# One kernel, one change: the second matrix of each expert as a single 4 MB load

## The chip, the cores and the metric

The kernel runs on one core of a Trainium2 chip. The metric is the time of one execution on the device in microseconds (us). Times of engines and transfers come from a hardware profile of one execution.

## What is computed

One decoder layer for 16 + 256 tokens of width 1024: attention and a state-space mixer side by side, gates, an output projection, and then the part that matters here, a layer of 32 experts of which every token takes 4. Cut to it:

```python
def moe_ffn(u, w_router, b_router, w1, b1, w2, b2):
    ...
    def body(acc, inp):
        tok, wt, e = inp
        hb = swiglu_clamped(u[tok] @ w1[e] + b1[e])     # w1[e]: 1024 x 2048
        yb = (hb @ w2[e] + b2[e]) * wt[:, None]         # w2[e]: 1024 x 1024
        return acc.at[tok].add(yb), None
```

`swiglu_clamped` takes the even columns of its input as one operand and the odd ones as the other, so 2048 columns give 1024 hidden units. All weights are float32: 8 MB for the first matrix of an expert, 4 MB for the second.

## The kernel before

Everything is held in SBUF: `ring`, 12 slots of 8 KB per partition, and `arena`, some 100 KB per partition. Each engine runs its own program; semaphores join them. All loads of weights are issued by SP, in one order written out by hand.

Up to about 480 us the kernel computes the projections, both mixers, the branch projections (`branch`, 12 groups counted by `branch_used`), the merged gates (`m_done`), the output projection (`wo_half` when its first half is through, `h_ready`) and the router. The weights of that part pass through slots 0 to 6 of the ring; slots 7 to 9 are scratch of the mixers and slots 10 and 11 hold the gates (`gsig`) until `m_done` is 8.

Then come the 32 experts in order, for up to 64 tokens each (`expert` of TensorE). An expert has six parts (`PARTS = 6`), each a load of 2 MB, that is 16 KB per partition (`BUF`): four parts of the first matrix (`w1_v`: part `s` has rows 256 s to 256 s + 255, two rows to a partition) and two halves of the second (`w2_v`: four rows to a partition). The first matrix has two sets of buffers: `even_bufs[0:4]` for even experts and `odd_bufs` for odd ones. The two halves of the second matrix have one buffer each, `even_bufs[4]` and `even_bufs[5]`, for all experts. After each part TensorE adds 1 to `slot_used`, six for an expert.

TensorE's order within an expert: bias, 4 parts of the first matrix (hidden units in two halves of 512, each in a PSUM bank), the gathering of a later expert's tokens (`gather`), the addition of the previous expert's result to the tokens (`scatter`), transposes of the hidden units, and the second matrix, half by half. A float32 matmul shows as two records; the two column halves of the array work in pairs, so a part of either matrix is 16 records.

SP's order: `first_experts` loads what is missing of expert 0, then the first matrix of expert 1. The loop then calls `step(e, ...)`, which fetches the first matrix of expert e + 1 (`doubled`, as its buffers, those of expert e - 1, are used) and then the second matrix of expert e (`single`, as that of expert e - 1 is used). At `TURN` = 20 the order changes (`in_order_of_use`): two parts of expert 21, the second matrix of 20, the other two parts of 21, the second matrix of 21; from there each expert's six parts in the order of use.

Of the kernel before, what the change touches and what calls it, by code (L numbers as in the profile page):

```python
# [25 lines left out]
P = 128  # L26
# [14 lines left out]
E = 32  # L41
# [14 lines left out]
PARTS = 6  # L56
# [34 lines left out]
def hybrid_layer(nc, x, meta, rel, g_mix, w_in, sinks, conv_w, conv_b, dt_bias, a_log, d_skip, g_ssm,  # L91
                 w_att, w_ssm, w_out, g_ffn, w_rt, b_rt, w1, b1, w2, b2, g_fin, c_sq, c_oh, out):
    ctx = ExitStack()
    with ctx:
# [27 lines left out]
        def at(off, *shape, dt=F32):  # L122
            n = int(np.prod(shape))
            words = n if dt != BF16 else n // 2
            v = arena[:, off:off + words]
            if dt != F32:
                v = v.bitcast(dt)
            if len(shape) == 1:
                return v
            names = "abcd"[:len(shape)]  # L130
            return v.rearrange(f"p ({' '.join(names)}) -> p {' '.join(names)}",
                               **{names[i]: shape[i] for i in range(len(shape))})
# [77 lines left out]
        def ring_pair(j):  # L210
            return ring[:, 2 * j:2 * j + 2, :].rearrange("p s w -> p (s w)")

        even_bufs = [at(6400, BUF), ring_pair(4), at(R, BUF), at(R + 6144, BUF), ring_pair(1), ring_pair(5)]
        odd_bufs = [ring_pair(3), ring_pair(2), ring_pair(0), at(0, BUF)]
        DOUBLED = range(len(odd_bufs))
        gfin, fin = odd_bufs[0][:, 0:D], odd_bufs[0][:, D:3 * D].rearrange("p (c d) -> p c d", c=2)
# [164 lines left out]
        def expert_buf(i, odd):  # L381

            if odd and i in DOUBLED:
                return odd_bufs[i], odd_loaded[i]
            return even_bufs[i], even_loaded[i]

        def expert_arrived(eng, i, t, pair, odd):
# [2 lines left out]
            eng.wait_ge(loaded, (pair if i in DOUBLED else t) * 16 + 16)  # L390

        w1_v = w1.rearrange("e (s p k) c -> e s p (k c)", p=P, k=2)
        w2_v = w2.rearrange("e (h p r) n -> e h p (r n)", p=P, r=4)

        def expert_sources(e, ahead=0):

            one = bass.ds(e, 1)
            src = [w1_v[ahead:][one, s].rearrange("e p f -> p (e f)") for s in range(4)]
            src += [w2_v[ahead:][one, h].rearrange("e p f -> p (e f)") for h in range(2)]
            return src  # L400

        G_PASS, EXP = E + 2, E + 1
# [4 lines left out]
        @block.sync  # L407
        def _(sp):
            sp.dma_start(xin[0:META, 0, :], meta).then_inc(x_in[0], 16)
            for c in range(2):  # L410
                sp.dma_start(xin[:, c + 1, :], x[c * P:(c + 1) * P, :]).then_inc(x_in[c + 1], 16)
            sp.dma_start(tab[0:NB, 0, :], rel).then_inc(rel_in, 16)
            sp.dma_start(ohs[0:NB + 1, :, :], c_oh).then_inc(rel_in, 16)

            def fetch(i, src, odd):
                dst, loaded = expert_buf(i, odd)
                if i >= 4:
                    dst = dst.rearrange("p (c f) -> p c f", c=2)
                sp.dma_start(dst, src).then_inc(loaded, 16)  # L419

            sources = expert_sources(0), expert_sources(1)
            for n, parts in enumerate(chunks):
                if n == ca[0] + FSLOTS + 1:

                    sp.wait_ge(y_done, 8)
                    for i in range(2):
                        fetch(i, sources[0][i], 0)
                if n == co[0]:
                    sp.wait_ge(tile_ready, T_END)
                    fetch(2, sources[0][2], 0)  # L430
                if n == co[2]:
                    sp.wait_ge(*released[held[FSLOTS - 1]])
                    fetch(0, sources[1][0], 1)
                if n >= FSLOTS:
                    sp.wait_ge(*released[before[n]])
                for dst, src in parts:
                    sp.dma_start(dst(slot_of[n]), src).then_inc(slot_loaded[slot_of[n]], 16)

            def first_experts():
                sp.wait_ge(branch_used, 12)  # L440
                fetch(3, sources[0][3], 0)
                fetch(4, sources[0][4], 0)
                sp.wait_ge(m_done, 8)
                fetch(5, sources[0][5], 0)
                sp.wait_ge(wo_half, 1)
                fetch(1, sources[1][1], 1)
                sp.wait_ge(h_ready, 3)
                for i in range(2, 4):
                    fetch(i, sources[1][i], 1)


            def doubled(sources, odd, used, parts=DOUBLED):

                for i in parts:
                    sp.wait_ge(slot_used, used + (i + 1))
                    fetch(i, sources[i], odd)

            def single(sources, odd, used):

                for i in range(DOUBLED.stop, PARTS):  # L460
                    sp.wait_ge(slot_used, used + (i + 1))
                    fetch(i, sources[i], odd)

            def step(e, odd, used):

                sources, following = expert_sources(e), expert_sources(e, 1)
                doubled(following, 1 - odd, used)
                single(sources, odd, used)

            TURN = 20

            def in_order_of_use(used):

                half = DOUBLED.stop // 2
                doubled(expert_sources(TURN + 1), (TURN + 1) % 2, used, range(half))
                single(expert_sources(TURN), TURN % 2, used)
                doubled(expert_sources(TURN + 1), (TURN + 1) % 2, used, range(half, DOUBLED.stop))
                single(expert_sources(TURN + 1), (TURN + 1) % 2, used + PARTS)  # L480
                for e in range(TURN + 2, E):
                    doubled(expert_sources(e), e % 2, used + PARTS * (e - TURN - 1))
                    single(expert_sources(e), e % 2, used + PARTS * (e - TURN))

            first_experts()
            PAIR = 2 * PARTS
            with sp.Fori(0, TURN // 2 - 1) as pair:
                step(pair * 2 + 1, 1, pair * PAIR)
                step(pair * 2 + 2, 0, pair * PAIR + PARTS)
            step(TURN - 1, 1, (TURN - 2) * PARTS)  # L490
            in_order_of_use((TURN - 1) * PARTS)
            sp.wait_ge(flag_ready, 1)
            more = sp.value_load(ofl[0:1, 0:1].bitcast(I32), min_val=0, max_val=1)
            with sp.If(more):
                with sp.Fori(0, PASSES - 1) as b:
                    doubled(expert_sources(0), 0, b * (E * PARTS) + (E - 2) * PARTS)
                    with sp.Fori(0, TURN // 2) as pair:
                        step(pair * 2, 0, b * (E * PARTS) + (pair * PAIR + (E - 1) * PARTS))
                        step(pair * 2 + 1, 1, b * (E * PARTS) + (pair * PAIR + E * PARTS))
                    in_order_of_use(b * (E * PARTS) + (E + TURN - 1) * PARTS)  # L500
                sp.wait_ge(slot_used, PASSES * E * PARTS - PARTS + 1)
            sp.wait_ge(slot_used, E * PARTS - PARTS + 1)
            sp.dma_start(gfin, bass.AP(g_fin.tensor, 0, [[0, P], [1, D]])).then_inc(gfin_in, 16)
            for c in range(2):
                sp.wait_ge(fin_ready, c + 1)
                sp.dma_start(out[c * P:(c + 1) * P, :], fin[:, c, :]).then_inc(out_done, 16)
            sp.wait_ge(out_done, 32)
# [770 lines left out]
        def _(pe):  # L1278
            tn = nc.tensor

            def mm(o, lhsT, rhs, first, last):
                return tn.matmul(o, lhsT, rhs, start=first, stop=last, skip_group_check=True)  # L1282
# [415 lines left out]
            def expert(t, b, pair, odd):  # L1698
                pe.wait_ge(b_ready, t + b + 1)

                bv = b1all.rearrange("p (h m c r) -> p h m c r", h=2, c=2, r=4)
                for half in range(2):
                    for c in range(2):
                        mm(bank[4 + half][64 * c:64 * c + 64, :], bsel[0:3 * E, :], bv[0:3 * E, half, :, c, :], True, False)
                pe.wait_ge(usel_ready, t + b + 1)
                for i in range(4):
                    expert_arrived(pe, i, t, pair, odd)
                    w = expert_buf(i, odd)[0].rearrange("p (k h m c r) -> p k h m c r", k=2, h=2, c=2, r=4)
                    for half in range(2):
                        for kk in range(2):  # L1710
                            k = 2 * i + kk
                            for c in range(2):
                                ins = mm(bank[4 + half][64 * c:64 * c + 64, :], usel[:, k, :], w[:, kk, half, :, c, :],
                                         False, k == KT - 1)
                        if i == 3 and half == 0:
                            ins.then_inc(hid_ready, 1)
                    ins.then_inc(slot_used, 1)
# [79 lines left out]
```

## Time and profile before

| | us |
|---|---|
| median of 3 runs | 1405.76 (1400.63 to 1406.92) |
| the profiled execution | 1401.74 |
| its span on the core | 1399.9 |
| TensorE (PE) busy | 1307.5, 93% of the span |
| VectorE, ScalarE, GpSimd busy | 390.9, 277.9, 43.2 |
| read from HBM | 466.61 MB, 334 GB/s over the span |
| granted TensorE clock, mean | 0.988 of 2.4 GHz |

A view "in order of time" lists groups of like instructions: start, time until the last one ends, engine, line, operation, output<-input, shape, count, and in brackets the idle time before them and what ended it. L1282 is a helper's line, in which all matmuls are recorded; L419 is the line in `fetch` from which all expert weights are loaded. A window A:B is given in us from the start of the span. DMA share is the mean busy share of 16 DMA engines; a packet that waits counts as busy, so the share can pass 1.00.

### The profile page before, as it was taken

How to read it: one execution, taken by the hardware profiler on the slowest of the kernel's cores; microseconds unless marked ns; L12 is line 12 of the kernel's file. 1: busy time of each engine (PE TensorE's matmuls, PEld its weight loads, DVE VectorE, ACT ScalarE, POOL GpSimd, SP SyncE). 2: the span in 40 equal slices, each digit the busy share in tenths (PEclk: the TensorE clock that was granted, in tenths of full speed). 3: DMA queues.
4: the chain of work that ended last, by engine and by line, in shares of the span. 5: the costliest groups of instructions: out<-in, count | busy, mean ns of one | idle time of the engine just before them, and what ended most of it. 6: DMA issues, size and time to landing. Idle time of an engine off the chain costs nothing.

```text
span 1399.9 us, 18601 instructions
## 1 busy us (share of the span) xinstructions
PE 1307.5 (93%) x7435; PEld 667.2 (48%) x7435; DVE 390.9 (28%) x942; ACT 277.9 (20%) x633; POOL 43.2 (3%) x48
## 2 busy tenths in 40 slices
PE   9999998999999999998989989999889999888996
PEld 5687787655886543343333333333333343333332
DVE  1055456677212531121111211112211221122112
ACT  3124325475100311111111111111111111111111
POOL 3000100020000000000000000000000000000000
PEclk9999999999999999999999999999999999999999
DMA  8733334353966599999999999999999999999995
GB/s 270 216 122 111 131 121 136 106 140 103 309 248 237 198 427 430 428 428 428 427 429 429 428 428 427 429 429 428 428 428 414 432 428 428 428 430 428 428 428 242
DMA packets 73871, 468.49 MB, mean 335 GB/s; under 512 B 4867, under 2 KB 37915, under 8 KB 49228
## 3 DMA queue, kind: packets, MB, share of 16 engines
q1 hardware_dynamic: 70444, 457.89, 80.7%
q0 software_dynamic: 1952, 5.61, 1.4%
q10 hardware_dynamic: 1440, 4.52, 0.9%
q8 instruction: 22, 0.36, 0.1%
q14 instruction: 13, 0.11, 0.0%
HBM read 466.61 MB, written 1.13 MB: 334 GB/s over the span
## 4 chain that ended last, share of the span: by engine, by line
PE 55%; DMA 38%; ACT 2%; DVE 2%; issue 1%; SPq 1%; POOL 0%; DVEq 0%; ACTq 0%; POOLq 0%
PE bank L1282 53%; DMA ring<-in_w 26%; DMA arena<-in_w 12%; DMA arena<-in_c_oh 1%; SPq L419 1%; PE bank L1394 0%; PE bank L1685 0%; ACT wdt L822 0%; ACT arena L737 0%; ACT arena L651 0%; PE bank L1324 0%; PE bank L1576 0%; DVE ring L981 0%; ACT arena L831 0%; DVE arena L1115 0%
## 5 line engine op out<-in xcount | busy, mean ns | idle before, releaser
L1282 PE MATMUL bank<-ring,arena 128*64 128x512 f32 (+3 forms) x2296 | 568.0, 603 | 55.2 <-DMA ring<-in_w 47.5
L1282 PEld LDWEIGHTS bank<-ring,arena 128*64 128x64 f32 (+2 forms) x2296 | 196.9, 144 | 384.1 <-issue 328.3
L1282 PE MATMUL bank<-arena 128*128 128x64 bf16 (+6 forms) x3052 | 358.1, 355 | 16.2 <-DMA arena<-in_w 13.1
L1282 PEld LDWEIGHTS bank<-arena 128*128 128x128 bf16 (+3 forms) x3052 | 173.4, 121 | 221.9 <-issue 190.0
L1282 PE MATMUL bank<-arena,ring 128*128 128x256 f32 (+2 forms) x1312 | 269.8, 385 | 2.5 <-ACT decays L643 1.6
L1282 PEld LDWEIGHTS bank<-arena,ring 128*128 128x128 f32 (+1 forms) x1312 | 217.2, 181 | 45.3 <-ACT decays L643 1.8
L1196 DVE TENSOR_SCALAR arena<-bank 128x256 f32<-128x256 f32 x64 | 27.1, 423 | 687.2 <-PE bank L1282 687.2
L827 ACT ACTIVATE arena<-arena 128x256 f32<-128x256 f32 x64 | 26.7, 417 | 418.5 <-DVE arena L1196 418.5
L834 ACT ACTIVATE arena<-bank 128x512 f32<-128x512 f32 x32 | 19.1, 597 | 276.8 <-PE bank L1282 276.8
L1282 PE MATMUL bank<-arena,wdt 64*128 64x512 f32 (+1 forms) x280 | 70.5, 603 | 1.7 <-issue 1.0
L827 ACT ACT_TABLE_LOAD x32 | 41.1, 1283 | 0.6
L522 POOL TENSOR_TENSOR rstd<-ssq,half_neg 128x1 f32<-128x1 f32 (+2 forms) x7 | 5.0, 714 | 1001.6 <-DVE ssq L1269 916.9
L1282 PEld LDWEIGHTS bank<-arena,wdt 64*128 64x128 f32 (+1 forms) x280 | 24.7, 181 | 22.7 <-issue 17.8
L822 ACT ACTIVATE wdt<-bank 128x256 f32<-128x256 f32 x32 | 12.3, 384 | 93.1 <-PE bank L1685 93.1
L1179 DVE TENSOR_SCALAR rows<-squares,arena 128x128 f32<-128x128 f32 x66 | 19.9, 344 | 35.9 <-PE bank L1685 35.9
L1198 DVE SCALAR_TENSOR_TENSOR arena<-arena 128x256 f32<-128x256 f32 x64 | 27.2, 425 | 2.2
L1200 DVE TENSOR_TENSOR arena<-arena 128x256 f32<-128x256 f32 x64 | 27.2, 425 | 2.2
L1197 DVE TENSOR_SCALAR arena<-bank 128x256 f32<-128x256 f32 x64 | 27.2, 425 | 2.2
L981 DVE SCALAR_TENSOR_TENSOR ring<-ring,cols 128x272 f32<-128x272 f32 x48 | 26.1, 543 | 1.7
L557 POOL TENSOR_TENSOR arena<-arena 128x1024 f32<-128x1024 f32 x8 | 18.9, 2363 | 215.0 <-DMA arena<-cum_rows 215.0
L979 DVE TENSOR_SCALAR ring<-ring,cols 128x272 f32<-128x272 f32 x24 | 13.3, 554 | 35.3 <-ACT ring L691 35.2
L1108 DVE TENSOR_TENSOR arena<-ring,bank 128x512 f32<-128x512 f32 x8 | 5.5, 687 | 61.2 <-PE bank L1282 61.1
(236 smaller groups left out, 594.5 us busy)
## 6 DMA issues: line engine op xcount, KB each, us to landing
ring<-in_w SPq DMA_DIRECT2D x128, 2048.0 KB, 25.3
arena<-in_w SPq DMA_DIRECT2D x64, 2048.0 KB, 29.2
ring<-in_w_in SPq DMA_DIRECT2D x34, 1024.0 KB, 6.2
ring<-in_w_ssm SPq DMA_DIRECT2D x8, 1024.0 KB, 7.7
arena<-cum_rows ACTq DMA_DIRECT2D x8, 512.0 KB, 5.3
ring<-in_w_att SPq DMA_DIRECT2D x16, 256.0 KB, 6.8
ring<-in_w_out SPq DMA_DIRECT2D x4, 1024.0 KB, 4.8
arena<-bias_rows POOLq DMA_DIRECT2D x1, 2048.0 KB, 11.4
```

The costliest lines, as they stand in the source:

```text
L419: sp.dma_start(dst, src).then_inc(loaded, 16)
L557: pool.tensor_tensor(cumbc[:, it % 2, :, :], cumbc[:, it % 2, :, :], smask.unsqueeze(1).to_broadcast([P, HPG, BLK]), ALU.add).then_inc(cum ...
L827: sc.activation(sig[:, half, :], glu[:, half, :], ACT.Sigmoid, scale=ALPHA).then_inc(esig_ready, 1)
L834: sc.activation(ysb, bank[6][:, :], ACT.Copy).then_inc(ye_saved, 1)
L979: ch.link(v.tensor_scalar(o, xp[:, 0:NT], w(0), col_cb[:, ct:ct + 1], ALU.mult, ALU.add))
L981: ch.link(v.scalar_tensor_tensor(o, xp[:, k:k + NT], w(k), o, ALU.mult, ALU.add))
L1179: ins = v.tensor_scalar(gwt[:, c, :], iota2, pos[:, c, bass.ds(col, 1)], wtok[:, c, bass.ds(col, 1)], ALU.is_equal, ALU.mult)
L1196: done(v.tensor_scalar(glu[:, half, :], hv[:, :, 0], LIMIT, None, ALU.min), glu_ready, t * 2 + half + 1)
L1197: ch.link(v.tensor_scalar(lin[:, half, :], hv[:, :, 1], -LIMIT, LIMIT, ALU.max, ALU.min))
L1198: ch.link(v.scalar_tensor_tensor(lin[:, half, :], lin[:, half, :], 1.0, glu[:, half, :], ALU.add, ALU.mult))
L1200: v.tensor_tensor(hsw[:, half, :], lin[:, half, :], sig[:, half, :], ALU.mult).then_inc(hs_ready, 1)
L1282: return tn.matmul(o, lhsT, rhs, start=first, stop=last, skip_group_check=True)
```

## The change

The second matrix of an expert becomes one transfer of 4 MB. `w2_v` gives each partition eight consecutive rows, one run of 32 KB. The destination is one buffer of 32 KB per partition, `second_buf`, in ring slots 8 to 11. So that this is one piece, part 1 of even experts moves from slots 8 and 9 to slots 2 and 3, where the first half was. Since partition p now holds hidden units 8 p to 8 p + 7, the units of a half are no longer the first or last 512, but groups of four in turn; TensorE reads first matrix and bias in runs of four elements at a pitch of 16 elements, before 8. In the queue: expert 0's part 1 is issued after part 3 and not in the branch stage, its second matrix when `m_done` is 8, and `single` waits until both halves of the previous second matrix are used (`used + PARTS`), where it waited for each half in turn.

```diff
--- before.py
+++ after.py
@@ -210,7 +210,9 @@
         def ring_pair(j):
             return ring[:, 2 * j:2 * j + 2, :].rearrange("p s w -> p (s w)")
 
-        even_bufs = [at(6400, BUF), ring_pair(4), at(R, BUF), at(R + 6144, BUF), ring_pair(1), ring_pair(5)]
+        even_bufs = [at(6400, BUF), ring_pair(1), at(R, BUF), at(R + 6144, BUF)]
+
+        second_buf = ring[:, 8:12, :].rearrange("p s w -> p (s w)")
         odd_bufs = [ring_pair(3), ring_pair(2), ring_pair(0), at(0, BUF)]
         DOUBLED = range(len(odd_bufs))
         gfin, fin = odd_bufs[0][:, 0:D], odd_bufs[0][:, D:3 * D].rearrange("p (c d) -> p c d", c=2)
@@ -382,6 +384,9 @@
 
             if odd and i in DOUBLED:
                 return odd_bufs[i], odd_loaded[i]
+            if i >= len(even_bufs):
+                half = i - len(even_bufs)
+                return second_buf[:, BUF * half:BUF * half + BUF], even_loaded[4]
             return even_bufs[i], even_loaded[i]
 
         def expert_arrived(eng, i, t, pair, odd):
@@ -390,13 +395,13 @@
             eng.wait_ge(loaded, (pair if i in DOUBLED else t) * 16 + 16)
 
         w1_v = w1.rearrange("e (s p k) c -> e s p (k c)", p=P, k=2)
-        w2_v = w2.rearrange("e (h p r) n -> e h p (r n)", p=P, r=4)
+        w2_v = w2.rearrange("e (p r) n -> e p (r n)", p=P)
 
         def expert_sources(e, ahead=0):
 
             one = bass.ds(e, 1)
             src = [w1_v[ahead:][one, s].rearrange("e p f -> p (e f)") for s in range(4)]
-            src += [w2_v[ahead:][one, h].rearrange("e p f -> p (e f)") for h in range(2)]
+            src += [w2_v[ahead:][one].rearrange("e p f -> p (e f)")]
             return src
 
         G_PASS, EXP = E + 2, E + 1
@@ -414,8 +419,8 @@
 
             def fetch(i, src, odd):
                 dst, loaded = expert_buf(i, odd)
-                if i >= 4:
-                    dst = dst.rearrange("p (c f) -> p c f", c=2)
+                if i == 4:
+                    dst = second_buf
                 sp.dma_start(dst, src).then_inc(loaded, 16)
 
             sources = expert_sources(0), expert_sources(1)
@@ -423,8 +428,7 @@
                 if n == ca[0] + FSLOTS + 1:
 
                     sp.wait_ge(y_done, 8)
-                    for i in range(2):
-                        fetch(i, sources[0][i], 0)
+                    fetch(0, sources[0][0], 0)
                 if n == co[0]:
                     sp.wait_ge(tile_ready, T_END)
                     fetch(2, sources[0][2], 0)
@@ -439,9 +443,9 @@
             def first_experts():
                 sp.wait_ge(branch_used, 12)
                 fetch(3, sources[0][3], 0)
+                fetch(1, sources[0][1], 0)
+                sp.wait_ge(m_done, 8)
                 fetch(4, sources[0][4], 0)
-                sp.wait_ge(m_done, 8)
-                fetch(5, sources[0][5], 0)
                 sp.wait_ge(wo_half, 1)
                 fetch(1, sources[1][1], 1)
                 sp.wait_ge(h_ready, 3)
@@ -457,9 +461,8 @@
 
             def single(sources, odd, used):
 
-                for i in range(DOUBLED.stop, PARTS):
-                    sp.wait_ge(slot_used, used + (i + 1))
-                    fetch(i, sources[i], odd)
+                sp.wait_ge(slot_used, used + PARTS)
+                fetch(4, sources[4], odd)
 
             def step(e, odd, used):
 
@@ -1698,19 +1701,19 @@
             def expert(t, b, pair, odd):
                 pe.wait_ge(b_ready, t + b + 1)
 
-                bv = b1all.rearrange("p (h m c r) -> p h m c r", h=2, c=2, r=4)
+                bv = b1all.rearrange("p (m h c r) -> p m h c r", h=2, c=2, r=4)
                 for half in range(2):
                     for c in range(2):
-                        mm(bank[4 + half][64 * c:64 * c + 64, :], bsel[0:3 * E, :], bv[0:3 * E, half, :, c, :], True, False)
+                        mm(bank[4 + half][64 * c:64 * c + 64, :], bsel[0:3 * E, :], bv[0:3 * E, :, half, c, :], True, False)
                 pe.wait_ge(usel_ready, t + b + 1)
                 for i in range(4):
                     expert_arrived(pe, i, t, pair, odd)
-                    w = expert_buf(i, odd)[0].rearrange("p (k h m c r) -> p k h m c r", k=2, h=2, c=2, r=4)
+                    w = expert_buf(i, odd)[0].rearrange("p (k m h c r) -> p k m h c r", k=2, h=2, c=2, r=4)
                     for half in range(2):
                         for kk in range(2):
                             k = 2 * i + kk
                             for c in range(2):
-                                ins = mm(bank[4 + half][64 * c:64 * c + 64, :], usel[:, k, :], w[:, kk, half, :, c, :],
+                                ins = mm(bank[4 + half][64 * c:64 * c + 64, :], usel[:, k, :], w[:, kk, :, half, c, :],
                                          False, k == KT - 1)
                         if i == 3 and half == 0:
                             ins.then_inc(hid_ready, 1)
```

## Rows read from the trace of the kernel before

**Rows 1.** The page: span, strip of 40 slices, queue q1.

```profile
span 1399.9 us, 18601 instructions
...
GB/s 270 216 122 111 131 121 136 106 140 103 309 248 237 198 427 430 428 428 428 427 429 429 428 428 427 429 429 428 428 428 414 432 428 428 428 430 428 428 428 242
...
q1 hardware_dynamic: 70444, 457.89, 80.7%
```

**Rows 2.** Windows: stretch, length, PE, PEld, DVE, ACT, POOL busy, PEclk, DMA share, GB/s.

```profile
502.00:528.00 26.00, 25.55 (x162) 10.15 (x162) 4.95 (x14) 3.64 (x8) 0.00 (x0) 1.00 1.00 427
...
692.00:721.40 29.40, 25.79 (x164) 11.05 (x166) 4.95 (x14) 3.65 (x7) 0.00 (x0) 1.00 1.01 429
...
580.00:1040.00 460.00, 420.04 (x2582) 168.44 (x2584) 77.77 (x219) 57.60 (x110) 0.00 (x0) 0.97 1.01 429
...
1100.00:1380.00 280.00, 256.96 (x1606) 97.15 (x1602) 48.79 (x138) 35.56 (x67) 0.00 (x0) 1.00 1.01 429
```

**Rows 3.** DMA issues: form, count, KB each, median us from issue to landing.

```profile
ring<-in_w SPq DMA_DIRECT2D x128, 2048.0 KB, 25.3
arena<-in_w SPq DMA_DIRECT2D x64, 2048.0 KB, 29.2
...
ring<-in_g_fin SPq DMA_DIRECT2D x1, 512.0 KB, 19.2
```

**Rows 4.** The DMA queue's own issues, 436 to 512 us.

```profile
438.37 2.38 SPq L419 DMA_DIRECT2D ring<-in_w  x2
...
455.16 17.50 SPq L419 DMA_DIRECT2D ring<-in_w  x2
...
487.27 0.36 SPq L419 DMA_DIRECT2D arena<-in_w  x1
...
505.90 3.77 SPq L419 DMA_DIRECT2D ring<-in_w  x2
```

**Rows 5.** Windows of 2 us before and at the start of the stream.

```profile
464.00:466.00 2.00, 1.84 (x9) 1.07 (x8) 0.57 (x3) 1.62 (x6) 0.40 (x1) 1.00 0.00 0
...
486.00:488.00 2.00, 2.00 (x12) 0.74 (x10) 1.93 (x3) 0.00 (x0) 0.00 (x0) 1.00 0.00 0
488.00:490.00 2.00, 2.00 (x12) 0.71 (x10) 1.93 (x3) 0.00 (x0) 0.00 (x0) 1.00 0.90 238
```

**Rows 6.** TensorE in order of time, expert 0's second matrix.

```profile
502.07 7.09 PE L1282 MATMUL bank<-ring,arena 128*64 128x512 f32 x32 [0.45 <-ACT arena L831]
```

**Rows 7.** TensorE in order of time, experts 18 and 19.

```profile
1014.98 3.65 PE L1282 MATMUL bank<-ring,arena 128*64 128x512 f32 x16 [2.12 <-DMA ring<-in_w]
1019.96 3.65 PE L1282 MATMUL bank<-ring,arena 128*64 128x512 f32 x16 [1.33 <-DMA ring<-in_w]
...
1023.88 10.50 PE L1282 MATMUL bank<-ring,arena 128*64 128x512 f32 x48
...
1044.33 8.79 PE L1282 MATMUL bank<-ring,arena 128*64 128x512 f32 x32 [2.24 <-DMA ring<-in_w]
```

**Rows 8.** The DMA queue's own issues at the turn and at the end.

```profile
1075.72 3.76 SPq L419 DMA_DIRECT2D ring<-in_w  x2
...
1364.86 0.34 SPq L503 DMA_DIRECT2D ring<-in_g_fin  x1
```

**Rows 9.** Windows: branch stage, after a wait, and the turn.

```profile
360.00:380.00 20.00, 20.00 (x104) 17.18 (x103) 1.26 (x8) 4.60 (x12) 0.53 (x1) 1.00 1.04 376
...
1044.30:1048.00 3.70, 3.67 (x10) 1.07 (x12) 0.00 (x0) 0.00 (x0) 0.00 (x0) 0.58 1.00 425
...
1076.00:1078.00 2.00, 2.00 (x12) 0.69 (x10) 0.00 (x0) 0.00 (x0) 0.00 (x0) 1.00 0.85 229
1078.00:1080.00 2.00, 2.00 (x14) 0.82 (x12) 0.00 (x0) 0.82 (x2) 0.00 (x0) 1.00 0.89 377
```

**Rows 10.** TensorE in order of time, the last expert.

```profile
1373.06 5.16 PE L1282 MATMUL bank<-arena 128*64 128x512 f32 x64 [1.95 <-DMA arena<-in_w]
...
1381.44 7.09 PE L1282 MATMUL bank<-ring,arena 128*64 128x512 f32 x32 [0.46 <-ACT arena L831]
```

## The prediction

> **What bounds the kernel.** I read the page's strip first. Up to about 490 us the DMA engines have room and TensorE is busy; from slice 14 on the traffic stands at 427 to 432 GB/s with one dent in slice 30 (414; the slices count from 0) [rows 1]. That stage is the 32 experts. The windows show two regimes in it. Where the expert's weights are already there, TensorE takes 26.0 us an expert (DMA share 1.00 all the same). Elsewhere an expert takes 29.4 us, with TensorE waiting for the difference, and the rate is 429 GB/s over 460 us and over 280 us [rows 2]. An expert is six transfers of 2 MB, all from line L419 [rows 3], 12.58 MB, and 12.58/0.4287 = 29.35 us: the period is the DMA's. So the end of the kernel is the start of this stream, plus its bytes over its rate, plus every moment in which the stream runs dry, plus what TensorE has left after the last landings. TensorE being 93% busy is no bound. The change has to be read against these four.
>
> **Start of the stream.** The queue's issues show where the load starts. Before expert 0 is computed all of its six parts and the first matrix of expert 1 are loaded, and then the buffers are full: no traffic in 486:488 [rows 5]. The stream begins with the first part of expert 2, issued at 487.27, after which the window 488:490 carries 238 of 428 GB/s, so data flows from 488.9: 1.6 us from issue to data [rows 4, 5].
> The change delays part 1 of expert 0 (one 2 MB load, 4.9 us) from the branch stage to just behind part 3 (438.4), and issues the 4 MB load where the last half was, at 440.4. Queued from there: 8 MB from about 439.7, thus until 459.3, then odd part 1 (issued 455.16) until 464.2. Nothing is transferred in 464:466 today, and part 1 of expert 0 is wanted only at about 487. The 4.9 us disappear in that hole: cost 0. Without the hole they would be 4.9 us.
>
> **First dry spell.** Expert 2's four parts last from 488.9 to 488.9 + 4 x 4.895 = 508.5. Today the first half of expert 1's second matrix is issued at 505.90, when the first half of expert 0's is used up, the other at 509.34 (505.90 + 3.77 - 0.33) [rows 4]: the queue never empties. With one buffer the fetch waits for both halves: 509.3, data from 510.9. Dry for 2.4 us. What SP holds behind this wait is expert 3's first matrix, which waits for later use anyway. TensorE doesn't feel it yet: it wants this matrix at 528 (502.07 + 26.0). But from the point at which the DMA is the bound, all stands 2.4 us later.
>
> **The steady loop.** Here the fetch of the next second matrix is issued 7.3 us after the landing of this one (502.07 to 509.34 for 32 records of matmul [rows 4, 6]). In front of it stands the first matrix of the expert after next, 19.6 us. No dry spell; cover left 12 us. TensorE now waits once, for all 4 MB: 29.4 - 26.0 = 3.4 us, where it waited 2.1 and 1.3 us with half of the work between [rows 7]. No loss in the period.
> There is one side effect. After a wait of 2.24 us at 1044.33 the 32 records take 8.79 us instead of 7.09 [rows 6, 7], and the granted clock is 0.58 there, so part of it at the lower level, 1.2 GHz [rows 9]: 1.7 us. A wait of 3.4 us can do it too. In the loop it only shortens the next wait (3.4 to 1.7 us). At the turn it counts: 0 to 1.7 us; I take 0.9, since of the waits before second matrices today some end in it and some don't.
>
> **The turn.** At expert 20 the order of issue changes: two parts of 21, second matrix of 20, the other two parts of 21, second matrix of 21. In front of each second matrix stand only two parts, 9.8 us. Today that is just too little: the second matrix of 21 is issued at 1075.72 [rows 8] and 1076:1080 carries 229 and 377 GB/s [rows 9], 1.2 us lost. With the change, step by step:
> expert 18's last half lands at 1019.96 [rows 7], expert 19's one period later, 1049.3; plus 2.4 is 1051.7. Used, and the next fetch issued, 7.3 us on: 1059.0, data 1060.6. The queue is empty before that: today it runs out at 1075.72 + 1.6 - 1.2 = 1076.1, which is six parts (29.4 us) after the end of expert 19's last half, 1046.7 (so 2.6 us lie between the last byte and the landing at 1049.3); with the change 1046.7 + 2.4 + 9.8 = 1058.9. Dry for 1.7 us. From there TensorE sets the pace: expert 20's matrix lands at 1060.6 + 9.8 + 2.6 = 1073.0 and is wanted at 1051.7 + 26.0 = 1077.7; it is used up and that of 21 issued at 1085.0, with the queue empty since 1080.2. Issue 1085.0 against 1075.72 is 9.3 us, first dry spell included, today's own dent taken off. From here to the end the stream is unbroken, so all 9.3 us reach the end. This is the main term.
> Would TensorE's catching up save any of it? No: the DMA is the bound again a few experts later, and what it has not moved by then it moves later.
>
> **The tail.** The last expert's first matrix ends its wait at 1373.06 and the second is begun at 1381.44 with no wait for a DMA [rows 10]. The gains for the final norm are issued at 1364.86 and land 19.2 us later, 1384.1 [rows 3, 8], 0.5 MB (1.2 us) behind the last half: 1382.8. Today that half is wanted only 3.5 us (half of 7.09) after 1381.44; one transfer must be complete at 1381.44: + 1.4 us.
>
> **The packets.** The same bytes come as 32 KB runs in place of two of 16 KB. The trace has no 32 KB packet. At 428.7 GB/s over 16 engines a 16 KB packet takes 611.5 ns. Queue q1 as a whole: 80.7% of 16 x 1399.9 us is 18075 us of engine time; the 24576 expert packets (192 x 128) are 15028 of it, leaving 3047 us for 45868 packets and 55.2 MB, 66 ns for 1204 B [rows 1, 3]. A straight line gives 23 ns fixed per packet. That is a ceiling, since small packets' times overlap (360:380 shows share 1.04 at 376 GB/s [rows 9]). So a 4 MB load, 8 pairs an engine, gains 0 to 0.18 us; 30 loads count: 0 to 5.5 us. I take a third, 1.8 us. For a loss nothing speaks but that larger was always better so far; as the other end I keep the same 5.5 us.
> A page puts the ceiling elsewhere. By the Trainium skill, DMA: Bandwidth & Descriptors, Where 436 GB/s comes from, the ports stop at 435.2 GB/s; an estimate from it is 0.15 us a load, 4.6 us in all, and the sum would be 2.8 us lower. The trace agrees as far as no slice is above 432.
>
> **The matmuls.** Operands of the first matrix are read as runs of 4 elements 16 apart, not 8. The trace has 8 apart (48 records in 10.50 us at 1023.88) and contiguous (32 in 7.09): 0.43 us a pair both [rows 6, 7]. The pitch cost nothing there; I take 0. The bias and the hidden order cost as many instructions as before. Cover: 3.4 us an expert. SP issues one DMA fewer per expert, 0.4 us on a queue that waits anyway.
>
> **Sum.** 9.3 + 0.9 + 1.4 - 1.8 = + 9.8 us. The profiled execution took 1401.74 us (1399.9 and 1.8 around it), which gives 1411.5; it lies 4.0 below the median 1405.76, with which the sum is 1415.6. I forecast between them, 1413.5.
>
> **Rivals.**
> 1. *The run length pays.* The ceiling of 5.5 us is reached and no low clock meets the turn: 9.3 + 1.4 - 5.5 = + 5.2, 1409. For it: per-packet cost is real. Against: steady packets already stand at 429 GB/s. Chance 0.15.
> 2. *Faster.* The stream's price per transfer is larger than I see, and 31 transfers fewer win it back. It decides from 11.6/30 = 0.39 us a load, that is 4 MB in 9.40 us, 446 GB/s; faster by 0.5% (7 us) takes 457. The best slice is 432 [rows 1]. The full form: each transfer exposes the 1.6 us that lie between issue and data, 31 x 1.6 - 11.6 = 38 us less, 1364 to 1368. Against: halves land 4.98 us apart [rows 7], and 2.10 MB at 429 GB/s is 4.89. A page states that form: by the Trainium skill, SBUF — State Buffer, The DMA setup-cost knee, a transfer costs about 2 us plus its bytes, so fewer and larger is better; an estimate from its figure is 62 - 11.6 = 50 us less. The trace disagrees for a queue that is kept full. Chance 0.07 (0.02 the full form).
> 3. *Longer packets are slower*, by a row pitch of 32 KB: + 9.8 + 1.8 + 5.5 = 17 us, 1419 to 1423. No row either way. Chance 0.12.
> 4. *TensorE becomes the bound* through the wider pitch: 3.4 us of cover over 13.7 us of first-matrix matmuls, so from 25% on; at double time (39.7 - 29.4) x 32 = 330 us, 1735. Chance 0.03.
> 5. *The queue change shows nothing*: the stream is late but the experts' lead swallows it, + 1.4 - 1.8, about 1403. Against: the lead is TensorE's, not the DMA's. Chance 0.05.
>
> **Numbers.** The forecast has 0.58 and by itself 1408 to 1419. No change can be told within 0.5% (7 us). The forecast is beyond that in most of its own range (0.48 of the 0.58), rivals 3 and 4 all, rival 1 a third: slower 0.69, same 0.23, faster 0.08. The range takes in rival 1's 1409 less the run's own 3 us of scatter and rival 3: 1405 to 1424.
>
> **What would show it.** Right: issues of 4 MB at about 509 and 1085, low GB/s at 508:511 and for some 5 us around 1082; one wait of 3.4 or 1.7 us before each second matrix between 640 and 1050; a period of 29.3; a wait of 1.4 us before the last second matrix. Wrong: a period under 29.1 or over 29.6 (packets), 0.43 us a pair not kept (pitch), traffic without a hole at 1080 (queue), or a hole in 440:490 that isn't there.

## The result and the profile after

The changed kernel takes 1414.71 us (median of 13 runs, 1408.46 to 1416.70) against 1405.76 us for the one before (13 runs, 1400.15 to 1406.92). The ratio is 1.0066 with a 95% interval of 1.0052 to 1.0079: slower by 9.3 us (7.3 to 11.1). The forecast was 1413.5 us, with a range of 1405 to 1424, and a sum of + 9.8.

The page of the changed kernel: span, the strip, queue q1.

```profile
span 1414.9 us, 18515 instructions
...
GB/s 276 206 119 119 119 121 133 104 130 108 247 245 251 243 404 430 429 435 425 429 429 429 434 426 429 429 432 431 427 428 311 432 429 430 430 430 429 430 429 225
...
q1 hardware_dynamic: 65836, 457.89, 79.4%
```

Against [rows 1]: the same bytes in 4608 packets fewer (32 x 128 long ones in place of 64 x 128, and 512 fewer small ones). The level of the stream is the same or a little higher (single slices reach 434 and 435), and slice 30, the turn, falls to 311 where it was 414. The slice at the start of the stream has 404, before 427.

The span is 15.0 us longer, not 9.3. The reader has to take off what is not the change's. The stream starts with the first part of expert 2; the queue's own issues of the changed kernel show it at the end of the row at 477.89 (477.89 + 14.52 - 0.34 = 492.07), against 487.27 in [rows 4]:

```profile
443.15 2.38 SPq L424 DMA_DIRECT2D ring<-in_w  x2
...
477.89 14.52 SPq L424 DMA_DIRECT2D arena<-in_w  x2
...
514.11 0.33 SPq L424 DMA_DIRECT2D ring<-in_w  x1
...
1064.06 0.80 SPq L424 DMA_DIRECT2D ring<-in_w  x2
...
1090.07 0.33 SPq L424 DMA_DIRECT2D ring<-in_w  x1
```

All of these 4.8 us arise before the first 260 us of the kernel before are over, in code that the change doesn't touch (last section); gentle_turn below, which is the changed kernel up to expert 20, starts the same matmuls at 501.21. The row at 443.15 is 4.8 us later than its like in [rows 4], the row at 514.11 is 4.8 later than 509.3. So I compare from the start of expert 0's second matrix to the end of expert 31's, "the expert stage": 1381.44 + 7.09 - 502.07 = 886.46 us before [rows 6, 10]; TensorE of the changed kernel in order of time gives 1396.41 + 7.09 - 506.85 = 896.65, that is 10.2 us more.

```profile
506.85 7.09 PE L1285 MATMUL bank<-ring,arena 128*64 128x512 f32 x32 [0.45 <-ACT arena L834]
...
1025.95 8.60 PE L1285 MATMUL bank<-ring,arena 128*64 128x512 f32 x32 [3.74 <-DMA ring<-in_w]
...
1034.85 10.47 PE L1285 MATMUL bank<-ring,arena 128*64 128x512 f32 x48
...
1082.95 7.09 PE L1285 MATMUL bank<-ring,arena 128*64 128x512 f32 x32 [0.46 <-ACT arena L834]
...
1386.33 6.86 PE L1285 MATMUL bank<-arena 128*64 128x512 f32 x64 [1.97 <-DMA arena<-in_w]
...
1396.41 7.09 PE L1285 MATMUL bank<-ring,arena 128*64 128x512 f32 x32 [0.46 <-ACT arena L834]
```

Windows of the changed kernel at the first hole, at the two holes of the turn, and after the wait for expert 19's second matrix (columns as in [rows 2]):

```profile
506.85:532.85 26.00, 25.56 (x162) 10.22 (x162) 4.94 (x14) 3.64 (x8) 0.00 (x0) 1.00 0.94 394
...
1050.00:1110.00 60.00, 56.88 (x353) 22.52 (x351) 12.07 (x36) 8.23 (x17) 0.00 (x0) 0.97 0.86 359
...
1055.30:1060.00 4.70, 4.70 (x16) 1.40 (x18) 0.00 (x0) 0.00 (x0) 0.00 (x0) 0.64 1.01 429
...
1062.00:1064.00 2.00, 2.00 (x12) 0.67 (x10) 0.00 (x0) 0.00 (x0) 0.00 (x0) 1.00 0.18 74
...
1084.00:1086.00 2.00, 2.00 (x13) 0.60 (x9) 0.00 (x0) 0.00 (x0) 0.00 (x0) 1.00 0.50 213
1086.00:1088.00 2.00, 2.00 (x12) 0.74 (x10) 0.00 (x0) 0.00 (x0) 0.00 (x0) 1.00 0.00 0
1088.00:1090.00 2.00, 2.00 (x12) 0.69 (x10) 0.00 (x0) 0.00 (x0) 0.00 (x0) 1.00 0.00 0
```

TensorE is busy in every one of these windows of 2 us, in two of which the DMA engines stand still altogether. That is what a starved load queue looks like from TensorE's side: nothing. The 26 us of the first window carry 394 in place of 427 GB/s, so 2.0 us are missing; the 60 us at the turn carry 359, where a stream without a hole (below) has 430: 60 x (1 - 359/430) = 9.9 us. These are estimates from the rates. The kernel before lost 1.2 us of its own at the turn.

### The profile page after: what moved, and what is told of

It reads as the page before. It is cut to its first block, busy times and chain, and to the rows that moved or that the text cites. A ratio compares the mean times of both kernels' runs of the same rounds, so it can differ in the third digit from the quotient of the medians.

```text
span 1414.9 us, 18515 instructions
## 1 busy us (share of the span) xinstructions
PE 1316.4 (93%) x7435; PEld 663.2 (47%) x7435; DVE 390.4 (28%) x942; ACT 278.0 (20%) x633; POOL 43.6 (3%) x48
## 4 chain that ended last, share of the span: by engine, by line
PE 56%; DMA 39%; ACT 2%; DVE 2%; issue 1%; SPq 0%; DVEq 0%; ACTq 0%; POOLq 0%; POOL 0%
PE bank L1285 54%; DMA ring<-in_w 36%; DMA arena<-in_w 3%; PE bank L1397 0%; ACT arena L740 0%; ACT arena L654 0%; PE bank L1327 0%; PE bank L1579 0%; DVE ring L984 0%; DVE arena L1118 0%; PE bank L1399 0%; PE bank L1688 0%; DVE arena L947 0%; ACT wdt L825 0%; SPq L424 0%
## 5 line engine op out<-in xcount | busy, mean ns | idle before, releaser
L1285 PEld LDWEIGHTS bank<-arena 128*128 128x128 bf16 (+3 forms) x3052 | 169.9, 121 | 225.0 <-issue 194.9
```

## The experiments

The theory A: the wait for the whole of the previous second matrix, and its landing as a whole, let the queue run dry at the start and at the turn. The rival B: the new layout costs the time (runs of 32 KB, or the matmuls' wider pitch). Smaller rivals stand with the runs. Times are compared with runs of the kernel before that were made alongside (medians 1405.56 and 1405.28). The ratio takes in all runs of both kernels, so it differs a little from the quotient of the medians. The expert stage is that of one profiled execution each, measured as above; it holds that execution's stretches at the lower clock:

| kernel | median us | ratio to before, 95% | expert stage us |
|---|---|---|---|
| before | 1405.76 | 1 | 886.46 |
| changed | 1414.71 | 1.0066 (1.0052 to 1.0079) | 896.65 |
| wait_alone | 1409.73 | 1.0040 (1.0027 to 1.0053) | 894.31 |
| two_loads | 1403.58 | 0.9996 (0.9983 to 1.0009) | 886.32 |
| one_load_16k | 1414.47 | 1.0075 (1.0056 to 1.0094) | 898.81 |
| one_load_8k | 1422.34 | 1.0130 (1.0101 to 1.0159) | 903.56 |
| gentle_turn | 1406.68 | 1.0011 (0.9997 to 1.0024) | 887.16 |
| sharp_turn | 1417.57 | 1.0097 (1.0074 to 1.0121) | 899.39 |
| two_loads_gentle | 1403.83 | 0.9989 (0.9974 to 1.0005) | 885.83 |
| before_gentle | 1404.54 | 0.9997 (0.9982 to 1.0012) | 885.77 |

**The wait without the new layout (wait_alone).** The kernel before with

```diff
+                sp.wait_ge(slot_used, used + PARTS)
                 for i in range(DOUBLED.stop, PARTS):
-                    sp.wait_ge(slot_used, used + (i + 1))
                     fetch(i, sources[i], odd)
```

> The kernel before with one edit: both 2 MB halves of a second matrix are fetched only when the whole of the previous second matrix is used. Theory A (the queue runs dry): dry for about 2.4 us at 508, and at the turn the second matrix of 21 is issued some 5.5 us later than in the kernel before; in all 5.5 to 6.5 us slower than the kernel before, no wait in the tail, period unchanged at 29.37 us. Theory B (the loss comes with the new layout, the 32 KB runs or the wider pitch of the matmuls): no change against the kernel before. If the wait is the whole cause of the loss, 9 us.

Measured: 0.40% or 5.6 us slower, and no wait for a DMA before the last second matrix. One window at the start and one at the turn, the turn's issue, and the matmuls ahead of the last second matrix, of this kernel:

```profile
500.00:526.00 26.00, 25.55 (x164) 10.15 (x162) 4.94 (x14) 3.65 (x7) 0.00 (x0) 1.00 0.94 390
...
1070.00:1090.00 20.00, 19.54 (x112) 7.68 (x110) 2.48 (x8) 2.81 (x5) 0.00 (x0) 1.00 0.81 329
...
1080.91 0.80 SPq L419 DMA_DIRECT2D ring<-in_w  x2
...
1378.52 6.86 PE L1282 MATMUL bank<-arena 128*64 128x512 f32 x64 [1.96 <-DMA arena<-in_w]
```

The issue at the turn is 5.2 us later than 1075.72 [rows 8] (5.9 with the 0.7 us by which this execution was ahead at expert 0, 501.38 against 502.07). The expert stage is 7.9 us longer; 1.7 of that is a stretch at the lower clock at 1378.52 (6.86 us in place of the 5.16 of [rows 10]), which leaves 6.2. B is wrong for more than half of the loss: old layout, old packets, and 5.6 us are there. But it isn't the whole: the halves still land and are worked through one by one.

**The layout without the wait (two_loads).** The changed kernel, loaded in halves of four rows per partition, each with its own wait:

```diff
-        w2_v = w2.rearrange("e (p r) n -> e p (r n)", p=P)
+        w2_v = w2.rearrange("e (p h r) n -> e h p (r n)", p=P, h=2)
...
-            src += [w2_v[ahead:][one].rearrange("e p f -> p (e f)")]
+            src += [w2_v[ahead:][one, h].rearrange("e p f -> p (e f)") for h in range(2)]
...
-                return second_buf[:, BUF * half:BUF * half + BUF], even_loaded[4]
+                return second_buf[:, BUF * half:BUF * half + BUF], even_loaded[i]
...
-                sp.wait_ge(slot_used, used + PARTS)
-                fetch(4, sources[4], odd)
+                for i in range(DOUBLED.stop, PARTS):
+                    sp.wait_ge(slot_used, used + (i + 1))
+                    fetch(i, sources[i], odd)
```

> The changed kernel with its new layout of the second matrix and of the first one's columns, but loaded as two transfers of 2 MB (16 KB runs, 32 KB apart), each with its own semaphore and its own wait as before. Theory A: as the kernel before within 1 us, period 29.37 us, a dent of about 1 us at the turn. Theory B: 8 to 10 us slower than the kernel before, as the changed one.

Measured: ratio 0.9996, expert stage 886.32 us against 886.46. The loss is gone although the columns of the first matrix are read at the wider pitch, the bias too, the rows of a half lie 32 KB apart in memory, and part 1 of expert 0 is loaded late. So the costs set at 0 (pitch, late load) show as nothing within the interval, which goes from 2.4 us faster to 1.3 us slower. This refutes one half of B. The other half, the runs of 32 KB, isn't in this kernel, whose runs are of 16 KB; the next two sections settle it.

**Shorter packets in one load (one_load_16k, one_load_8k).** The first puts the 4 MB down in two places, slots 2 and 3 and slots 10 and 11 (part 1 of even experts goes back to slots 8 and 9):

```diff
-        second_buf = ring[:, 8:12, :].rearrange("p s w -> p (s w)")
+        second_buf = ring[:, 2:12, :].rearrange("p (a s) w -> p a (s w)", s=2)[:, 0:5:4, :]
+        second_half = [ring_pair(1), ring_pair(5)]
...
-                    dst = second_buf
+                    dst, src = second_buf, src.rearrange("p (a f) -> p a f", a=2)
```

> The changed kernel with the 4 MB transfer put down in two places of 16 KB per partition, so one transfer, one wait, but packets of 16 KB. Theory A (the shorter period comes from fewer packets): period 29.37 us in place of 29.29, 2.0 to 2.3 us slower than the changed kernel. Rival C (it comes from fewer transfers): period 29.29, the time of the changed kernel.

The second takes slots 2, 5, 8 and 11, one by one. Two buffers of first matrices move for it, and of expert 0's loads part 1 and the second matrix each wait for one event more:

```diff
-        second_buf = ring[:, 8:12, :].rearrange("p s w -> p (s w)")
-        odd_bufs = [ring_pair(3), ring_pair(2), ring_pair(0), at(0, BUF)]
+        second_buf = ring[:, 2:12:3, :]
+        odd_bufs = [two_slots(6), two_slots(3), two_slots(0), at(0, BUF)]
...
-                    dst = second_buf
+                    dst, src = second_buf, src.rearrange("p (a f) -> p a f", a=4)
```

> The changed kernel with the 4 MB transfer put down in four places of 8 KB per partition (ring slots 2, 5, 8 and 11, other buffers moved for it), so packets of 8 KB: 32 per engine and load in place of 8. Theory A (each packet carries a fixed price; from the periods of 29.29, 29.37 and 29.37 us for 8, 16 and 16 packets it is 9 to 10 ns): period 29.50 to 29.53 us, 6 to 7 us slower than the changed kernel. Rival: only packets over 16 KB gain or the price is not per packet: period 29.37, 2 us slower than the changed kernel.

The period is read from two second matrices whose start waits for the DMA, 14 experts apart (15 in wait_alone). TensorE in order of time, the changed kernel:

```profile
615.83 8.78 PE L1285 MATMUL bank<-ring,arena 128*64 128x512 f32 x32 [3.72 <-DMA ring<-in_w]
...
1025.95 8.60 PE L1285 MATMUL bank<-ring,arena 128*64 128x512 f32 x32 [3.74 <-DMA ring<-in_w]
```

one_load_16k:

```profile
615.04 8.53 PE L1286 MATMUL bank<-ring,arena 128*64 128x512 f32 x32 [3.81 <-DMA ring<-in_w]
...
1026.16 7.09 PE L1286 MATMUL bank<-ring,arena 128*64 128x512 f32 x32 [2.12 <-DMA ring<-in_w]
```

one_load_8k:

```profile
613.31 8.49 PE L1288 MATMUL bank<-ring,arena 128*64 128x512 f32 x32 [3.96 <-DMA ring<-in_w]
...
1026.65 7.09 PE L1288 MATMUL bank<-ring,arena 128*64 128x512 f32 x32 [2.27 <-DMA ring<-in_w]
```

and wait_alone, with two loads of 2 MB in 16 KB packets, by its second halves:

```profile
610.71 3.65 PE L1282 MATMUL bank<-ring,arena 128*64 128x512 f32 x16 [1.33 <-DMA ring<-in_w]
...
1051.21 3.65 PE L1282 MATMUL bank<-ring,arena 128*64 128x512 f32 x16 [1.33 <-DMA ring<-in_w]
```

Periods 410.12/14 = 29.294, 411.12/14 = 29.366 and 413.34/14 = 29.524 us for 8, 16 and 32 packets per engine and load, and 440.50/15 = 29.367 for two loads. That is 9.0 and 9.9 ns for each packet more, so at these lengths the same price for each packet. Rival C (fewer transfers, not fewer packets) is out, since one_load_16k makes one transfer and has the period of two. The periods also show that runs of 32 KB don't cost time: the one with them is the shortest. By time, one_load_8k is 1.0130/1.0066, some 9 us, slower than the changed kernel, a little more than the 6 to 7 expected, which lie within the intervals; its expert stage is 6.9 us longer. Between one_load_16k and the changed kernel the ratios can't tell 1 us from 3; the stages differ by 2.2.

**The turn (gentle_turn, sharp_turn).** The changed kernel with the order from expert 20 on written as a list of how many parts stand ahead of each second matrix:

```diff
-                half = DOUBLED.stop // 2
-                doubled(expert_sources(TURN + 1), (TURN + 1) % 2, used, range(half))
-                single(expert_sources(TURN), TURN % 2, used)
-                doubled(expert_sources(TURN + 1), (TURN + 1) % 2, used, range(half, DOUBLED.stop))
-                single(expert_sources(TURN + 1), (TURN + 1) % 2, used + PARTS)
-                for e in range(TURN + 2, E):
-                    doubled(expert_sources(e), e % 2, used + PARTS * (e - TURN - 1))
+                ahead = {TURN: 3, TURN + 1: 2, TURN + 2: 1, TURN + 3: 1}
+                parts = [(e, i) for e in range(TURN + 1, E) for i in DOUBLED]
+                done = 0
+                for e in range(TURN, E):
+                    upto = min(len(parts), 4 * (e - TURN) + ahead.get(e, 0))
+                    for n, i in parts[done:upto]:
+                        doubled(expert_sources(n), n % 2, used + PARTS * (n - TURN - 1), (i,))
+                    done = upto
                     single(expert_sources(e), e % 2, used + PARTS * (e - TURN))
```

> The changed kernel with another order of loads from expert 20 on: 3, 3, 3, 4, 3 parts of first matrices in front of the second matrices of 20 to 24 where it had 2, 2, 4, 4, 4. Theory A: the holes at the turn (about 1.5 and 7 us) close, 7.5 to 9.5 us faster than the changed kernel, 0 to 1.5 us slower than the kernel before. Rival D (TensorE's pace at the turn, not the empty queue, costs the time, or the holes only move): less than 3 us faster than the changed kernel.

sharp_turn has `ahead = {}`.

> The changed kernel with a sharper turn: no part of a first matrix between the second matrices of 19 and 20, then four each. Theory A: one hole of 11 us right behind the second matrix of 19, none at the next; 2 to 4 us slower than the changed kernel. Rival D (the holes don't add up to the loss): no difference, or faster since one of the two holes is gone.

The window of the turn in gentle_turn:

```profile
1050.00:1110.00 60.00, 59.08 (x366) 22.91 (x362) 9.87 (x28) 8.76 (x16) 0.00 (x0) 1.00 1.01 430
```

and the one hole of sharp_turn, behind the second matrix of 19:

```profile
1046.00:1050.00 4.00, 3.06 (x25) 1.58 (x20) 2.23 (x8) 0.94 (x3) 0.00 (x0) 1.00 0.63 270
1050.00:1054.00 4.00, 2.92 (x14) 1.06 (x16) 0.00 (x0) 0.00 (x0) 0.00 (x0) 1.00 0.00 0
1054.00:1058.00 4.00, 4.00 (x21) 1.27 (x19) 0.00 (x0) 0.00 (x0) 0.00 (x0) 1.00 0.00 0
1058.00:1062.00 4.00, 4.00 (x24) 1.50 (x22) 0.00 (x0) 1.88 (x2) 0.00 (x0) 1.00 0.76 262
```

gentle_turn is 1.0011 of the kernel before, so 7.7 us faster than the changed kernel (9.5 in the expert stage), with the same TensorE work, the same single buffer and the same runs of 32 KB. Rival D is out: holes closed are time returned. What was left of B is out with it. In sharp_turn some 11 us are missing in the four windows, expected was a hole of 11; it is 1.0097/1.0066, 4 us, slower than the changed kernel, expected were 2 to 4, but by the two intervals anything from about 0.5 to 8 is possible.

**The version the experiments point to (two_loads_gentle), and its control (before_gentle).** The first is two_loads with the turn of gentle_turn, the second the kernel before with it.

> Two loads of 2 MB with their own waits in the new layout, with the order of 3, 3, 3, 4, 3 parts from expert 20 on. Theory A: no hole anywhere in the stream, 0.5 to 1.5 us faster than two loads with the old turn, and 1 us faster than the kernel before. Rival: the old dent of 1.2 us is not the queue's, no difference.

> The kernel before, with nothing changed but the order of 3, 3, 3, 4, 3 parts from expert 20 on. Theory A: 0.5 to 1.5 us faster than the kernel before (its dent of 1.2 us closes). Rival: the gain of the gentler turn seen on the changed kernel is a gain of its own and not the closing of the holes: some 8 us faster here too.

The dent of the turn closes in both: the window 1070:1080 carried 377 GB/s in the kernel before, here 429 and 426. The stages are 0.6 and 0.7 us shorter than before, the ratios 0.9989 and 0.9997 with intervals that hold 1. So the two profiles show about half a microsecond less, at the low end of what was expected, and by the runs no difference can be told. That before_gentle doesn't gain some 8 us rules out its rival: the gentler order has no gain of its own apart from the holes that it closes. No version here beats the kernel before beyond doubt.

## Why the prediction was right

Of the expert stage's 10.2 us, point by point, with the 4.8 us of the first 260 us taken off every time:

- **Late first load, 0.** Right. The stream starts 4.8 us later, as does the issue in front of it at 443.15; two_loads loses nothing by it.
- **First dry spell, 2.4.** Right. Issue at 514.11 - 4.8 = 509.3, as worked out; 2.0 us of bytes are missing in the window around it, and it is there in wait_alone too. TensorE felt it only later: expert 1's second matrix was begun at 532.87 with no wait for a DMA, 26.02 us after expert 0's.
- **Steady loop, nothing lost.** Right: one wait per expert, 3.7 us or, after a stretch at the lower clock, 2.0 to 2.2; the 0.46 us for ScalarE that other rows show is in it.
- **Packets, - 1.8 (0 to - 5.5).** Right in sign and near in size, and now measured: 0.072 us a load, 2.2 us over 30. The ceiling of 23 ns per packet taken from the queue's mean was 2.5 times the price of 9; that a third of it was taken was a guess that came out well. The port limit that the Trainium skill gives (DMA: Bandwidth & Descriptors, Where 436 GB/s comes from) was not reached over any long stretch: the changed kernel has 429 GB/s in 640:1040 and 430 in 1200:1380.
- **The turn, 9.3 with the first spell, + 0.9 for the clock.** Right in size and mechanism. Second matrix of 20 issued at 1064.06 - 4.8 = 1059.3 (worked out: 1059.0), that of 21 at 1090.07 - 4.8 = 1085.3 (1085.0), 9.6 us after that of the kernel before. That these agree to 0.3 us is in part luck, since two parts differ and cancel: 19 shorter loads had brought the stream forward by 1.4 us, which the working put into another term, and the low clock did meet expert 19 in this execution, with all its 1.7 us (0.64 in the window behind 1055.3; 27.71 us to the next second matrix in place of 26.01). Of the five profiles with one load of 4 MB three met it there (8.78, 8.44 and 8.78 us) and two didn't (7.09), so 0.9 was a fair middle. The holes themselves are measured by gentle_turn.
- **The tail, 1.4.** Right as a wait, but not in every execution. In gentle_turn and one_load_16k (the rows below) the last second matrix starts after a wait for the DMA of 1.79 and 1.87 us, of which 0.46 is ScalarE's as ever: 1.3 and 1.4 us. In the profile of the changed kernel the matmuls ahead of it ran partly at 1.2 GHz (6.86 us at 1386.33 in place of 5.16 in [rows 10]) and took 1.7 us from TensorE's side instead; the wait had nothing left to show.

```profile
1381.28 7.09 PE L1286 MATMUL bank<-ring,arena 128*64 128x512 f32 x32 [1.79 <-DMA ring<-in_w]
```

```profile
1397.30 7.09 PE L1286 MATMUL bank<-ring,arena 128*64 128x512 f32 x32 [1.87 <-DMA ring<-in_w]
```

- **Matmul pitch, 0.** Right: 48 records in 10.47 us, before 10.50.

The sum was + 9.8, against 9.3 by the ratio (7.3 to 11.1) and 10.2 in the stage. With the sizes that this execution had, it is 9.3 + 1.7 + 1.7 - 2.2 = 10.5; by the bytes missing in the windows, an estimate, it is 2.0 + 9.9 - 1.2 + 1.7 - 2.2 = 10.2. The forecast of 1413.5 lay halfway between the sum on the profiled execution and on the median; measured were 1414.71, against the 1415.6 that the sum gave on the median.

wait_alone and one_load_16k split the loss by the ratios: 5.6 us for the later issue, another 4.9 for the landing in one piece (10.5 in all; the layout, which differs too between these two, costs nothing by two_loads), and - 1.2 for the long packets. The last two are differences of two ratios, each uncertain by some 3 us. The stages give 7.9 (with 1.7 of lower clock in it), 4.5 and - 2.2, the periods - 2.2 for the packets. The rivals: the run length did pay, but 2 us, not 5.5; the full price per transfer is not there, as one transfer in place of two left the period at 29.37 us. By the Trainium skill's rule (SBUF — State Buffer, The DMA setup-cost knee) one load of 4 MB should beat two of 2 MB; in a queue that is kept full no run shows such a gain.

## What to carry to other kernels

In a stage bound by loads, ask of every merge of two buffers: when can the next load be issued, and is there enough in front of it in the queue until then? Count it at the start of the stream and wherever the order of loads changes, not in the steady loop, which may have 12 us to spare while the turn has none. Longer packets bought 2 us; waits and landings twice as coarse cost some 10; and the cheapest repair was not a buffer but an order of loads that changes by one part at a time.

## What the runs showed beyond that

**Three groups of times in one kernel.** The 64 runs of the kernel before fall into 1400.2 to 1401.8 us (18 runs), 1402.4 to 1404.0 (9) and 1405.0 to 1407.0 (37); the 12 of two_loads into 1400.6 to 1401.2, 1403.5 to 1403.7 and 1405.4 to 1406.0. The profiles show where it can come from. Windows of the kernel before, of before_gentle and of the changed kernel, in a stage where all three run the same code:

```profile
220.00:240.00 20.00, 16.50 (x80) 13.05 (x79) 10.78 (x21) 11.35 (x28) 2.36 (x1) 1.00 0.37 130
240.00:260.00 20.00, 17.28 (x80) 13.39 (x79) 15.03 (x26) 10.83 (x28) 2.36 (x1) 1.00 0.39 131
```

```profile
220.00:240.00 20.00, 16.50 (x73) 12.71 (x72) 11.08 (x21) 11.08 (x28) 2.34 (x1) 0.91 0.37 131
240.00:260.00 20.00, 17.28 (x80) 13.43 (x79) 14.62 (x25) 10.71 (x27) 2.35 (x1) 1.00 0.37 131
```

```profile
220.00:240.00 20.00, 16.50 (x66) 12.49 (x65) 11.05 (x21) 11.03 (x27) 2.34 (x1) 0.84 0.38 131
240.00:260.00 20.00, 17.28 (x73) 12.91 (x73) 13.34 (x22) 10.25 (x27) 2.35 (x1) 0.93 0.39 131
```

TensorE waits 3.5 and 2.7 us in these windows in all three, but the clock stays at 2.4 GHz in the first, is at 1.2 GHz for a part of one window in the second, and for a part of both in the third, with 14 and 7 records fewer done than in the first. The ten profiles fall into the same three kinds. Before, wait_alone and gentle_turn have 1.00 twice and start expert 0's second matrix at 501.2 to 502.1 us. before_gentle, sharp_turn and one_load_8k have 0.91 and 1.00 and start at 503.0 to 503.6. The changed kernel, two_loads, two_loads_gentle and one_load_16k have 0.83 or 0.84 and 0.91 or 0.93 and start at 505.6 to 506.9. gentle_turn, with the changed code, is among the early. No profile of the old layout is among the late, but 37 of the 64 runs of the kernel before are in its latest group of times. That the same code does all three is shown; that it makes the groups of run times is inferred from the like steps of some 2 us each. What decides it in an execution is open.

**Whether a wait ends in the lower clock** did not follow its length alone: a wait of 2.21 us before expert 19's second matrix did in the changed kernel (the matmuls took 8.78 us), while 2.12 us before that of expert 18 in one_load_16k did not (7.09).
